# Two transformer blocks on one core: the last block's entry with squares summed by TensorE, the shift on ScalarE, and two projection groups that share each input tile

## The reference, cut to what matters

```
h = h + 0.5 * rms_norm(f, ln_ffn2[i, 1])           # f: the last feed-forward of the first block
x = h[:, N_META:]                                  # 256 tokens, 1024 features
mod = jax.nn.silu(c) @ w_mod[l] + b_mod[l]         # six vectors of 1024: sh_m, sc_m, gt_m, sh_f, sc_f, gt_f
h = rms_norm_2(x, g_mix_norm[l]) * (1.0 + sc_m) + sh_m
proj = h @ w_in[l]                                 # q_a k_a v_a q_i k_i w_i q_b k_b v_b gate_a gate_b
q_i = apply_rope(q_i); k_i = apply_rope(k_i)       # index queries (8 heads of 64) and the index key
score = einsum(w_i, relu(q_i . k_i)); sel = top_k(score, 64)
o_a = attention over sel;  o_b = attention over blocks
merged = sigmoid(gate_a) * (o_a @ w_br_dsa) + sigmoid(gate_b) * (o_b @ w_br_moba)
x = x + gt_m * (merged @ w_out[l])                 # then a gated feed-forward
```

## Time and profile before

| what | value |
|---|---|
| median of 3 runs | 1466.49 us (1465.28 to 1468.98) |
| span of the profiled execution | 1468.2 us; no other time of this execution is listed |
| TensorE busy | 1446.1 us, 98% |
| weight loads | 1406.6 us, 96% |
| VectorE, ScalarE busy | 1056.6 us (72%), 700.0 us (48%) |
| granted TensorE clock, mean | 0.998 of full speed |
| end of `down 3`, start of `rows(0)` | about 1054.9 us, 1092.33 us |

### The profile page before, as it was taken

How to read it: one execution, slowest core, us unless ns; L and a number is a source line. 1 busy time by engine, 2 the same in 40 slices (tenths; PEclk the granted TensorE clock), 3 DMA queues, 4 the chain that set the end, 5 groups by cost and what they waited for, 6 DMA issues and landing times. The chain is left out here.

```text
span 1468.2 us, 28465 instructions
## 1 busy us (share of the span) xinstructions
PE 1446.1 (98%) x11585; PEld 1406.6 (96%) x11585; DVE 1056.6 (72%) x1439; ACT 700.0 (48%) x910; POOL 29.0 (2%) x58
## 2 busy tenths in 40 slices
PE   8999999999999999999999999999999999999999
PEld 8999999999999999999999889999987899999999
DVE  6766779777667786677878768767887777876652
ACT  6544353454443454443554655443436766544431
POOL 0000100000001000001000000001000000000000
PEclk9999999999999999999999999999999999999999
DMA  9555835437447644458343226647633436365540
GB/s 324 220 187 186 268 149 201 172 106 267 172 172 249 239 173 172 171 196 288 128 173 124 78 70 246 227 173 268 234 115 135 145 139 231 131 228 185 184 173 30
DMA packets 42538, 269.09 MB, mean 183 GB/s; under 512 B 4768, under 2 KB 5920, under 8 KB 13520
## 3 DMA queue, kind: packets, MB, share of 16 engines
q1 hardware_dynamic: 33984, 240.31, 45.1%
q0 software_dynamic: 7312, 26.44, 5.5%
q10 hardware_dynamic: 1152, 1.05, 0.2%
HBM read 266.73 MB, written 1.05 MB: 182 GB/s over the span
## 5 line engine op out<-in xcount | busy, mean ns | idle before, releaser
L418 PE MATMUL ps<-x_hi,w_hi 128*128 128x272 f32 (+2 forms) x2296 | 661.8, 288 | 6.7 <-DVE x_lo L1447 1.9
L420 PE MATMUL ps<-x_hi,w_lo 128*128 128x272 f32 (+2 forms) x2296 | 651.8, 284 | 0.0
L419 PE MATMUL ps<-x_lo,w_hi 128*128 128x272 f32 (+2 forms) x2296 | 651.7, 284 | 0.0
L2024 ACT ACTIVATE w_hi<-raw_weights 128x2048 fp32r<-128x2048 f32 x219 | 416.9, 1912 | 291.6 <-PE ps L420 289.0
L1174 DVE TENSOR_TENSOR w_lo<-raw_weights,w_hi 128x2048 fp32r<-128x2048 f32 x193 | 439.7, 2288 | 143.8 <-ACT w_hi L2024 143.3
L418 PEld LDWEIGHTS ps<-x_hi,w_hi 128*128 128x128 f32 x2296 | 433.1, 189 | 10.8 <-DVE x_lo L1380 2.5
L419 PEld LDWEIGHTS ps<-x_lo,w_hi 128*128 128x128 f32 x2296 | 433.3, 189 | 0.7
L420 PEld LDWEIGHTS ps<-x_hi,w_lo 128*128 128x128 f32 x2296 | 433.1, 189 | 0.0
L418 PE MATMUL ps<-a_hi,w_hi 128*128 128x272 f32 x592 | 169.6, 286 | 0.0
L419 PE MATMUL ps<-a_lo,w_hi 128*128 128x272 f32 x592 | 169.6, 286 | 0.0
L420 PE MATMUL ps<-a_hi,w_lo 128*128 128x272 f32 x592 | 169.6, 286 | 0.0
(11 more groups left out here) (259 smaller groups left out, 1543.9 us busy)
## 6 DMA issues: line engine op xcount, KB each, us to landing
raw_weights<-w_units SPq DMA_DIRECT2D x226, 1024.0 KB, 4.9
mod_w<-mod_units POOLq DMA_DIRECT2D x48, 512.0 KB, 5.5
raw_weights<-w_units SPq DMA_DIRECT2D x4, 256.0 KB, 5.8
raw_weights<-w_units SPq DMA_DIRECT2D x2, 512.0 KB, 9.2
out<-h ACTq DMA_DIRECT2D x8, 128.0 KB, 1.9
h<-x_in SPq DMA_DIRECT2D x2, 272.0 KB, 4.1
h<-x_in SPq DMA_DIRECT2D x1, 544.0 KB, 8.0
tab<-tables POOLq DMA_DIRECT2D x1, 512.0 KB, 7.9
```

Of the source, the lines that this page charges most:

```text
L418: pe.matmul(dst, wh, hi, start=start, stop=False)
L419: pe.matmul(dst, wh, lo, start=False, stop=False)
L420: return pe.matmul(dst, wl, hi, start=False, stop=stop)
L2024: act.activation(w_hi[:, u % RING, :], raw[:, u % RING, :], ACT.Copy).then_inc(S["hi_ready"], 1)
```

## The change

Entry, on TensorE: the filler of 60 and the second `stats` are gone. `entry_sums` goes over the eight tiles of x and for each issues two fillers, one column of modulation sums, then, when ScalarE's square of that tile is ready, two one-column sums straight from the square into banks 2 and 3. VectorE no longer adds these squares. Spread and modulation banks of this stage move to 0 and 1. `entry_groups` takes the small group and the index-query group together: each input tile is used for all six output tiles, and the first tile's high products start before its low part is there.

On VectorE and ScalarE: VectorE multiplies by the spread value, ScalarE applies gain and shift, waits for its own result and copies the high part. ScalarE evicts the index queries (`store_qi`) in place of VectorE.

Later in `w_in`: `key_and_weights` and the index jobs move to later places, the two `turn_rows(0, .)` too. The attention of the selected keys (`scores2(4)` on) starts two places later. Of the first `take_best`, two rounds instead of five come before `row_rope(0, .)` and six instead of three behind it.

```diff
         def mod_bank(st):
-            return (st.t0 + st.shift + 6) % 8
+            return 1 if st.name == "w_in" else (st.t0 + st.shift + 6) % 8
         def spread_bank(st):
-            return (st.t0 + st.shift + COPIED - 1) % 8
+            return 0 if st.name == "w_in" else (st.t0 + st.shift + COPIED - 1) % 8
...
-            stats(stages["down", 3], w_in, filler=60)
-            stats(stages["down", 3], w_in, evict=False, filler=10)
-
-            def small_group():
+            def entry_sums():
+                for m in range(KT):
+                    keep_busy(w_in, 2)
+                    mod_sum(m)
+                    pe.wait_ge(S["sq_ready"], c.up("sq_ready"))
+                    for n, at_token in enumerate(starts(SEQ)):
+                        ins = pe.matmul(ps[:, 2 + n, 0:1], sq[:, m % 2, at_token:at_token + P], ones[:, 0:1],
+                                        start=m == 0, stop=m == KT - 1)
+                    if m != KT - 2:
+                        ins.then_inc(S["sq_used" if m < KT - 2 else "stats_done"], 1)
+                c.up("std_ready")
+                for n in range(8, 10):
+                    mod_sum(n)
+                    keep_busy(w_in, 1)
+                spread(SEQ, spread_bank(w_in))
+                for n in range(10, 12):
+                    keep_busy(w_in, 4)
+                    mod_sum(n)
...
+            def entry_groups():
...
+                pe.wait_ge(S["x_hi_ready"], X0["w_in"] + 1)
+                for m in range(2):
+                    hi_passes(*small(0, m), x_hi[:, 0, 0:SEQ])
+                for m in range(GROUP):
+                    hi_passes(*query(0, m), x_hi[:, 0, 0:SEQ])
                 for k in range(KT):
...
+                        ins = three_pass(*small(k, m), x_hi[:, k, 0:SEQ], x_lo[:, k, 0:SEQ], False, k == KT - 1)
...
+                    for m in range(GROUP):
+                        ins = three_pass(*query(k, m), x_hi[:, k, 0:SEQ], x_lo[:, k, 0:SEQ], False, k == KT - 1)
...
-            small_group()
-            group(w_in, 0, xs, between={1: [lambda: key_and_weights()]})
+            entry_groups()
             rows(0, {
-                0: [lambda: rotate_qi(0)], 1: [lambda: rotate_qi(1)], 2: [lambda: turn_tab(0)],
-                3: [lambda: idx_scores(0)], 4: [lambda: turn_tab(1)], 6: [lambda: idx_scores(1)]})
-            rows(1, {0: [lambda: turn_tab(2)], 1: [lambda: turn_tab(3)], 2: [lambda: idx_scores(2)]})
-            rows(2, {2: [lambda: turn_rows(0, 0)], 4: [lambda: turn_rows(0, 1)]})
+                0: [lambda: key_and_weights()], 1: [lambda: turn_tab(0)], 3: [lambda: rotate_qi(0)],
+                5: [lambda: turn_tab(1)], 6: [lambda: rotate_qi(1)]})
+            rows(1, {
+                0: [lambda: turn_tab(2)], 1: [lambda: idx_scores(0)], 2: [lambda: turn_tab(3)],
+                3: [lambda: idx_scores(1)], 5: [lambda: idx_scores(2)]})
+            rows(2, {3: [lambda: turn_rows(0, 0)], 6: [lambda: turn_rows(0, 1)]})
             rows(3, {2: [lambda: turn_rows(1, 0)], 5: [lambda: turn_rows(1, 1)]})
...
             paired(w_in, 8, xs, between={
-                3: [lambda: scores2(4)],
-                5: [lambda: scores2(5), lambda: turn_p2(4)], 6: [lambda: values2(4)],
-                7: [lambda: scores2(6), lambda: turn_p2(5)]})
+                5: [lambda: scores2(4)],
+                7: [lambda: scores2(5), lambda: turn_p2(4)]})
             paired(w_in, 9, xs, between={
-                0: [lambda: values2(5)],
-                1: [lambda: scores2(7), lambda: turn_p2(6)], 2: [lambda: values2(6)],
-                4: [lambda: turn_p2(7)], 5: [lambda: values2(7)]})
+                0: [lambda: values2(4)],
+                1: [lambda: scores2(6), lambda: turn_p2(5)], 2: [lambda: values2(5)],
+                3: [lambda: scores2(7), lambda: turn_p2(6)], 4: [lambda: values2(6)],
+                6: [lambda: turn_p2(7)], 7: [lambda: values2(7)]})
...
-                    if m >= 2 and nx is not None:
-                        add_square(m - 2, T, last)
+                    if m >= 2 and nx is not None and deferred:
+                        add_square(m - 2, T)
...
-                        dve.tensor_scalar(f[:, k, 0:T], f[:, k, 0:T], next_gain[:, k:k + 1], shift[:, k:k + 1],
-                                          ALU.mult, ALU.add).then_inc(S["full_ready"], 1)
...
+            mod_evict(3, mod_bank(w_in))
             split_to(u0 + 4)
-            mod_evict(3, 2)
-            dve.wait_ge(S["tile_done"], w_in.t0 + 4)
...
-            store(0, qi)
+            dve.wait_ge(S["roped"], 1)
             rotation(work1, 1, qi, 0)
             low_half()
+            low_half()
             rotation(work1, 1, qi, 1)
             low_half()
+            low_half()
             idx_add(0)
...
-            take_best(0, TOPK // 8 - 3)
+            take_best(0, 2)
...
-            take_best(0, 3)
+            take_best(0, TOPK // 8 - 2)
...
                         act.wait_ge(S["full_ready"], c.up("full_ready"))
+                        act.activation(f[:, m, 0:T], f[:, m, 0:T], ACT.Identity, scale=gain2[:, m:m + 1],
+                                       bias=mod[:, m:m + 1]).then_inc(S["full_kept"], 1)
+                        act.wait_ge(S["full_kept"], m + 1)
                         act.activation(hi[:, m, 0:T], f[:, m, 0:T], ACT.Copy).then_inc(S["x_hi_ready"], 1)
...
+            def store_qi(pair):
+                act.wait_ge(S["tile_done"], w_in.t0 + GROUP + 2 * pair + 2)
+                act.activation(qi[:, 2 * pair:2 * pair + 2, :], ps[:, GROUP + 2 * pair:GROUP + 2 * pair + 2, 0:SEQ], ACT.Copy)\
+                   .then_inc(S["tile_evicted"], 4)
```

More of the change, by code:

```diff
@@ L580, in keep_busy @@
             def keep_busy(st, n):
-                bank = st.bank(st.t0 + 3)
+                bank = mod_bank(st) if st.name == "w_in" else st.bank(st.t0 + 3)
                 for _ in range(n):
@@ L964, in bank7_free @@
+                    if k == 3:
+                        ins.then_inc(S["weights_used"], 1)
+            stats(stages["down", 3], w_in, filler=0)
+            entry_sums()
             def bank7_free():
+                pe.wait_ge(S["tile_evicted"], w_in.evicted(w_in.t0 + 2 * GROUP))
                 for name, n in (("v_stored", c.now("turned")), ("rotation_read", c.now("rotated")),
@@ L1354, in update_and_prepare @@
                 deferred = shift is None
-                last = 7 if deferred else 6
                 hi, lo = x_hi, x_lo
@@ L2075, in gate_up, with square @@
                 gated(n, 10)
-            def square(m, src, T):
+            def square(m, src, T, by_pe=False):
                 if m >= 2:
-                    act.wait_ge(S["sq_used"], c.now("sq_used") + max(1, m - 2))
+                    act.wait_ge(S["sq_used"], c.now("sq_used") + (m - 1 if by_pe else max(1, m - 2)))
                 act.activation(sq[:, m % 2, 0:T], src, ACT.Square).then_inc(S["sq_ready"], 1)
```

78 lines of the change are left out of this document (42 added, 36 removed).

## The result

The changed kernel takes 1485.01 us (median of 4 runs, 1479.94 to 1489.71) where the kernel before takes 1466.85 in the same comparison (4 runs, 1465.28 to 1468.98). The ratio is 1.0107, with an interval of 1.0088 to 1.0126 (the quotient of the two medians is 1.0124, inside it). The change makes the kernel slower, as forecast, but by about twice the 8.1 forecast.

The account below looks back on a forecast made before the run. TensorE, busy 98% of the span, was taken as the bound: -5.6 + 3.7 + 7.0 + 3.0 = +8.1, giving 1474.6 us. The forecast's own range was 1471.5 to 1478, widened to 1468.0 to 1479.5.

Parts of the forecast that it names:

- Step 1, the entry: Entry up to turn_rows(1, 0): earlier root and first product, modulation columns out of the products; 5.6 gained.
- TensorE keeps the pace: Entry sums: squares, two fillers and one modulation column take 0.9 to 1.0 per tile against 0.86; 0.1 late taken.
- R2: Rival, entry: lighter filling keeps the clock low for a second stretch, root some 1.6 later; +9.7, 1476.2, chance 0.15.
- Step 2: At turn_rows(1, 0): later index jobs make VectorE finish row_rope(1, 0) late, so TensorE waits; 3.7 lost.
- Step 3: Gate groups 8 to 10: later attention jobs delay VectorE's evictions, so TensorE waits for banks; 7.0 lost, bounds 5 and 9.
- the five parts: Waits from gate group 8 to the branch products: 0.6 for low weights, then 3.65, 1.1, 0.7 and 0.95 for evictions.
- Step 4: Clock falls behind the waits of 3.7 and 3.65, 1.5 lost for each; 3.0 lost, bounds 0 and 5.

Follow-up runs that it names:

- the eighth kernel: Changed kernel with more fillers and no modulation columns among the sums, old attention places and six take_best(0) rounds moved; 1470.99 us, ratio 1.0004 to the kernel before.
- e1_fill: Changed kernel with ten fillers instead of two ahead of the first square's sums; 1484.36 us, ratio 1.0102 to the kernel before.
- e6_all: Changed kernel with ten fillers ahead of the first square, old attention places and six take_best(0) rounds moved into VectorE's idle time; 1470.11 us, ratio 0.9992.
- e7_mod_back: Changed kernel with ten fillers first, three per tile behind, more around the spread, and twelve modulation columns back between the products; 1484.13 us, ratio 1.0088.
- e12_last: Kernel of e9 with two more modulation columns ahead of the first square and one more take_best(0) round moved back; 1465.74 us, ratio 0.9976 to the kernel before.
- e2: Changed kernel with six rounds of take_best(0) moved from before row_rope(1, 0) to three places where VectorE was idle; 1480.93 us, ratio 1.0070.
- e3: Changed kernel with the attention jobs of gate groups 8 and 9 back at their old places; 1476.77 us, ratio 1.0050.
- e5: Changed kernel with 28 fillers on TensorE ahead of turn_rows(1, 0), in its wait for VectorE; 1483.44 us, ratio 1.0085.
- e10: Kernel before with only the attention jobs of gate groups 8 and 9 moved two places later; 1480.44 us, ratio 1.0064.
- e4: Changed kernel with VectorE adding the second norm's squares again, 52 fillers and modulation columns in the wait; 1482.96 us, ratio 1.0086.
- e8: Same run as the eighth kernel: entry of e7 with old attention places and six take_best(0) rounds moved; 1470.99 us, ratio 1.0004 to the kernel before.
- e9: The eighth kernel with four modulation columns among the fillers around the spread and key_and_weights one place later; 1467.08 us, ratio 0.9979 to the kernel before.

## Why the prediction was right in its direction and wrong in its size

**What bounds the kernel: right.** Every cost found is a wait of TensorE or a time in which TensorE is slow.

**Step 1, the entry: wrong.** The step that failed is the sentence "TensorE keeps the pace", with its term of 0.9 to 1.0 per tile. At full clock the pace is there: 0.85 in the eighth kernel, whose second root is at 10.43 and first product at 13.34 behind T0, where the forecast had 11.1 and 13.85 (1067.2 and 1069.95 less 1056.10). But with a modulation column and two fillers around the sums the clock was at half from 1059.3 to 1076.3, and a tile took 1.55. Measured at TensorE's arrival at `turn_rows(1, 0)` the entry lost 0.64 (86.43 less the wait of 3.58 is 82.85, against 82.21), where the forecast had it 5.6 earlier than before. That is 6.2 of the 8.0 that were missing. The columns "cost nothing as long as the pace above holds", and it was they, with the thin filling, that broke it (e1_fill and e6_all against e7_mod_back, where both were altered at once; which of the two weighs more was not separated).

Nor did any kernel here reach the 5.6. In e12_last, with the clock at full speed throughout, TensorE is at `turn_rows(1, 0)` 3.2 earlier than before (79.21 less its wait of 0.21, against 82.21): six columns stand between the products again, so that 18.4 pass from the first product to `rows(0)` where the forecast had 16.4, and 47.2 from there instead of 46.4.

**R2 was the right mechanism with the wrong price.** It had the clock low for a second stretch and priced it at 1.6, since I took a length from the one fall seen before. The root came 4.6 later than forecast (15.72 for 11.1). In the changed kernel, and in e2, e3 and e5, the low stretch lasted from before the sums into the products. Nothing in the trace of before bounded its length, so the price should have been bounded by the whole entry at half speed.

**Step 2: right.** 3.58 for 3.7. `idx_add(0)` starts 19.9 behind `rows(0)` (20.15 forecast), and from there to the end of `row_rope(1, 0)` VectorE takes 29.8 (29.9 forecast); e2 removes it by moving work out of that list alone.

**Step 3: right in its order, a little low in its sum.** The waits are 0.78, 3.54, 0.94, 0.64 and 0.40, together 6.3, against a sum of 7.0 for the five parts. Yet from `scores2(0)` to `w_out` the kernel loses 9.2: 6.1 of idle time (6.3 less 0.2 that stood before), 1.7 of clock, and 1.4 that no row over 0.25 shows. Something like this 1.4 goes with the moved jobs. e10 loses 9.1 on that stretch. In e1_fill and e7_mod_back, where the clock does not fall here, the stretch takes 112.3 against 104.5 before, with 6.1 and 6.5 more idle time, so 1.7 and 1.2 are without a row; with the old places it takes 104.4 to 104.6 in every kernel. What it is made of was not found.

**Step 4: right in kind, low by 1.4.** I took 1.5 for each wait. Behind the first the clock was down for 6.8 and cost 2.7, as e5 shows by filling the wait; behind the second it was 3.4 and cost 1.7. The price is not a constant, and that a single 1.5 came so near was partly luck. Behind the same wait of 3.58 at `turn_rows(1, 0)`, `scores2(0)` follows after 10.5 in e1_fill and e7 and after 11.9 in the changed kernel, a price of 1.3 for 2.7; the same wait of 3.53 to 3.54 ahead of group 9 was followed by no fall in e1_fill and e7, and by one that cost 3.4 in e2 and e4 (the missing part of the granted clock, summed over the windows). The bounds 0 and 5 held. The page "TensorE: Matmul & The Clock Gate" of the Trainium skill, section "HAM oscillation — how this bites in real kernels", tells of streams that stop and start; both falls behind waits agree with it, and the missing fall in e1_fill and e7 does not. The entry went further than it: in e1_fill the clock fell at 1065.4 with TensorE's busy share at 1.00 on either side, so no stop that the profile shows was needed.

**The sum.** 0.64 + 3.58 + 2.7 + 6.1 + 1.7 + 1.4 = 16.1, against 16.17 on the ruler. Nothing is lost or won behind `w_out` (216.3 and 216.1 to the end of the span). The forecast's 8.1 lacks 6.2 of the entry, 1.4 of the clock and the 1.4 without a row, and has 1.0 too much in the two waits of steps 2 and 3.

One more small term: on ScalarE the pass with gain and shift takes 0.60, not the 0.42 that I took from the earlier trace rows:

```profile
1073.97 0.60 ACT L2164 ACTIVATE f<-f,mod,gain 128x256 f32<-128x256 f32 x1 [2.19 <-DVE f L1438]
1074.60 0.42 ACT L2167 ACTIVATE x_hi<-f 128x256 fp32r<-128x256 f32 x1
```

The cycle on ScalarE is 0.94 instead of 0.8 and stays hidden; it delays the first product by 0.2. The Trainium skill has it in "ScalarE: Activation LUTs", section "What ACT_TABLE_LOAD costs", which gives 186 ns and 0.833 ns an element, and 93 ns more for each of scale and bias that is read from memory; by it the pass would be an estimated 0.585, and the row above has 0.60.

## What to carry to other kernels

Where a stall is filled with real but tiny products in place of fillers, ask first whether the clock will hold, and price the doubt at the whole stretch at half speed, not at the length of the last fall: here twelve one-column products in place of fillers, with few fillers beside them, turned a forecast gain of 5.6 into a loss of 0.6, and the best entry tried gained 3.2. Read the clock column and the count of instructions beside the busy share. And when jobs move on one engine only, work out for each whose result its neighbours in the other engine's list wait for: two places later on TensorE put VectorE's eviction behind a softmax that had not begun, and that cost 9.2, more than the entry was forecast to give.

## What the runs showed of the hardware

**One-column products and the clock.** With sums, one modulation column and two fillers per tile the clock fell in all six kernels that had them, whether the idle time at T0 was 0.40 (e5_fill_wait), 1.77 (the changed kernel) or 3.33 (e6_all). With sums and three fillers per tile it held in e8, e9 and e12 (idle 0.41 to 0.53 at T0) and in e7, behind 3.13 of idle time, it fell once and came back during the sums. The nearest pair is e6_all and e7_mod_back: ten fillers ahead of the first square in both, idle time of 3.33 and 3.13 at T0, the clock down and back by 1064.5 in both; in e6_all it fell again at 1067.8, in e7 it held. All of this is one profiled execution for each kernel. The whole stretch of sums, root and groups in e12_last, in one window:

```profile
1056.00:1090.00 34.00, 33.98 (x279) 30.95 (x280) 19.56 (x45) 16.88 (x33) 0.00 (x0) 1.00 0.17 64
```

**Two paces at the same granted clock.** The same stretch of the first block, with the same instructions, in the kernel before (first fence) and in e9_best (second):

```profile
1000.00:1020.00 20.00, 20.00 (x179) 20.00 (x178) 15.50 (x22) 7.76 (x5) 2.44 (x5) 1.00 0.72 239
```

```profile
1000.00:1020.00 20.00, 20.00 (x172) 20.00 (x171) 15.74 (x23) 8.82 (x6) 2.49 (x5) 1.00 0.73 256
```

179 products in 20 us, or 172, both with TensorE busy throughout and the clock column at 1.00. T0 is at 1056.10 in the one and at 1061.69 in the other, though the code up to there is the same. The same two counts appear in the windows from 1420 to 1460 of other executions (172 in the changed kernel, 179 in e1_fill, where the end comes 3.1 sooner behind `w_out`). What chooses between them was not found. Single executions of one kernel spread over 5 to 10 us here (e9_best: 1463.1 to 1473.6), and this can be a part of it; it is why the experiments were read on a stretch of the trace and not on the total alone.
